# Attention exponents turned in 32x32 blocks by VectorE and through DRAM, instead of by TensorE

## The reference, cut to what matters

```
s_win = jnp.where(valid, s_win, -jnp.inf)
logits = jnp.concatenate([sink_logits(sink, s_win.shape[:-1]), s_ctx, s_win], axis=-1)
p = jax.nn.softmax(logits, axis=-1)
p_ctx = p[..., 1:1 + C].astype(v.dtype)
p_win = p[..., 1 + C:].astype(v.dtype)
return (jnp.einsum('bkgqj,bjkd->bqkgd', p_ctx, v_ctx)
        + jnp.einsum('bkgqj,bjkd->bqkgd', p_win, vw))
```

## Time and profile before

| | |
|---|---|
| median of 3 runs (range) | 1417.44 us (1417.28 to 1417.67) |
| profiled execution, span from first to last instruction | 1416.2 us |
| the runs' median less that span | 1.2 us |
| the attention with the z projection, first scores to last attended block | 383.8 to 657.8 us |
| busy over the whole span: TensorE, weight load, VectorE, ScalarE | 98%, 82%, 61%, 36% |
| mean granted TensorE clock | 0.999 of full speed |

### The profile page before, as it was taken

How to read it: one execution, slowest core, us unless ns; L and a number is a source line. 1 busy time by engine, 2 the same in 40 slices (tenths; PEclk the granted TensorE clock), 3 DMA queues, 4 the chain that set the end, 5 groups by cost and what they waited for, 6 DMA issues and landing times.

```text
span 1416.2 us, 19552 instructions
## 1 busy us (share of the span) xinstructions
PE 1389.8 (98%) x7474; PEld 1166.9 (82%) x7474; DVE 861.2 (61%) x1359; ACT 515.2 (36%) x798; POOL 74.6 (5%) x144
## 2 busy tenths in 40 slices
PE   4999999999999999999999999999999999999998
PEld 2788888888888888888888888888888888887887
DVE  6545655656778676776546685677666334474434
ACT  5323422244556444454222342122363223323332
POOL 0001111011100000000100101000000000010000
PEclk9999999999999999999999999999999999999999
DMA  9996567656712121224766656356523333365323
GB/s 384 407 390 245 184 212 243 195 183 207 223 46 64 56 75 52 67 89 132 234 188 190 197 181 214 92 165 193 177 90 105 92 102 91 106 203 182 111 89 119
DMA packets 64169, 232.75 MB, mean 164 GB/s; under 512 B 7120, under 2 KB 8144, under 8 KB 62816
## 3 DMA queue, kind: packets, MB, share of 16 engines
q1 hardware_dynamic: 42624, 154.23, 32.8%
q0 software_dynamic: 19792, 72.39, 16.3%
q10 hardware_dynamic: 1680, 5.10, 1.1%
HBM read 227.50 MB, written 4.19 MB: 164 GB/s over the span
## 4 chain that ended last, share of the span: by engine, by line
PE 92%; DVE 3%; DMA 2%; ACT 2%; SPq 1%; issue 1%; POOL 0%; POOLq 0%; DVEq 0%; ACTq 0%
PE ps L1439 90%; PE ps L1668 2%; DMA kvmem<-in_ctxT 1%; DMA modchunk<-in_modb 1%; DVE w_lo L857 1%; SPq L370 0%; ACT w_hi L452 0%; DVE modchunk L863 0%; ACT scratch L557 0%; DVE kvmem L1038 0%; PE ps L1793 0%; DVE pt_lo L1174 0%; ACT pt_hi L668 0%; ACT main L801 0%; DVE main L957 0%
## 5 line engine op out<-in xcount | busy, mean ns | idle before, releaser
L1439 PE MATMUL ps<-h_hi,w_hi 128*128 128x512 f32 x1592 | 625.8, 393 | 2.2 <-DVE w_lo L857 1.2
L1439 PE MATMUL ps<-h_hi,w_lo 128*128 128x512 f32 x1592 | 618.8, 389 | 0.0
L1439 PE MATMUL ps<-h_lo,w_hi 128*128 128x512 f32 x1592 | 618.4, 388 | 0.0
L857 DVE TENSOR_TENSOR w_lo<-raw,w_hi 128x1024 fp32r<-128x1024 f32 x206 | 252.3, 1225 | 372.3 <-ACT w_hi L452 372.0
L452 ACT CAST w_hi<-raw 128x1024 fp32r<-128x1024 f32 x206 | 216.1, 1049 | 600.2 <-PE ps L1439 599.9
L1439 PEld LDWEIGHTS ps<-h_hi,w_hi 128*128 128x128 f32 x1592 | 299.0, 188 | 65.7 <-issue 4.7
L1439 PEld LDWEIGHTS ps<-h_hi,w_lo 128*128 128x128 f32 x1592 | 298.9, 188 | 62.8
L1439 PEld LDWEIGHTS ps<-h_lo,w_hi 128*128 128x128 f32 x1592 | 299.2, 188 | 58.7
L863 DVE CUSTOM_DVE_ANT_0 modchunk<-modchunk,cond_row 128x1024 f32<-128x1024 f32 x128 | 154.6, 1220 | 22.2 <-DMA modchunk<-in_modb 22.0
L408 POOL DMA_DIRECT2D modchunk<-in_modb x128 | 67.9, 530 | 1114.9 <-DVE modacc L863 1090.9
L668 ACT CAST pt_hi<-ps 128x512 fp32r<-128x512 f32 (+1 forms) x48 | 30.7, 640 | 110.7 <-PE ps L1668 110.7
(11 more groups left out here) (232 smaller groups left out, 1364.5 us busy)
## 6 DMA issues: line engine op xcount, KB each, us to landing
raw<-in_weights SPq DMA_DIRECT2D x208, 512.0 KB, 3.6
modchunk<-in_modb POOLq DMA_DIRECT2D x128, 512.0 KB, 4.7
raw<-in_mod SPq DMA_DIRECT2D x32, 512.0 KB, 9.0
modchunk<-in_mod SPq DMA_DIRECT2D x16, 512.0 KB, 7.4
cond_row<-in_mod SPq DMA_DIRECT2D x16, 512.0 KB, 8.8
main<-in_xT SPq DMA_DIRECT2D x4, 1024.0 KB, 8.3
main<-in_xT ACTq DMA_DIRECT2D x4, 1024.0 KB, 5.0
out<-pooled SPq DMA_DIRECT2D x16, 256.0 KB, 2.8
```

The lines of the kernel that those rows point to most:

```text
L857: nc.vector.tensor_tensor(low, src, high.bitcast(F32), ALU.subtract).then_inc(lo_ready, 1)
L1439: return nc.tensor.matmul(out, lhsT, rhs, start=start, stop=stop, skip_group_check=True)
```

## The change

- TensorE's `turn` is gone, with the identity matrix and its load. In its place VectorE turns the exponents in 32x32 blocks (`turn_blocks`) into `blocks_out`; SP stores them to a DRAM buffer (one transfer of 128 rows of 2048 or 2560 bytes), waits until the store has landed, and fetches them back with four transfers, so that the 32x32 blocks come to their places of the full transpose (each 32 partitions with four runs of 512 or 640 bytes). High and low parts are then made from SBUF (`turned_hi`, `turned_lo`), three slots after the exponent (`TURN_LAG = 3`) instead of one.
- The exponents are not multiplied with the reciprocal of their sum. The row sums of a query block are inverted together (`invert_sums`, 128x3), sent through DRAM and fetched back as a row broadcast to all partitions, and the attended block is multiplied with it when it is copied out of PSUM (`block_out`).
- A head has 16 slots. `attend` is in the slots 6, 9, 12 and 15, with one bank unit ahead of it, and none behind the last. The next head's keys are prepared in slot 12 and its first scores are made in slot 14. The loops over heads are written out.
- `cond_row` and a part of `modchunk` serve as block buffers. POOL stores one row of `cond_row` to DRAM, and fetches it back to all partitions after the last step; chunk loads wait for that and for the last attended block, and the eight jobs of the first output group are spread as 0, 1, 1, 1, 2, 1, 1, 1.
- Beside the last head 8 of 16 input tiles are split instead of 12. Swaps and rotations of the last query tiles are moved into the first two heads, and reloads of x are later.

```diff
+SLOTS = 16
+UNIT_SLOTS = (2, 4, 6, 8, 10, 12, 13)
+BANK_STEPS = (2,) * 11 + (3, 3, 2, 2, 0)
+BLOCK_SLOTS = (6, 9, 12, 15)
+TURN_LAG = 3
+NEXT_KEYS, NEXT_SCORES = 12, 14
...
+            def store_blocks(i, k):
+                g, cols = i * STEPS + k, key_tiles(k) * P
+                sp.wait_ge(turned, g + 1)
+                sp.dma_start(turn_scratch[g % 4, :, 0:cols], blocks_out[g % 2][:, 0:cols]).then_inc(written[g % 2], 16)
+
+            def fetch_blocks(i, k):
+                g, cols = i * STEPS + k, key_tiles(k) * P
+                run = cols // 4
+                sp.wait_ge(written[g % 2], 16 * (g // 2 + 1))
+                if g >= 2:
+                    sp.wait_ge(pt_ready, g - 1)
+                for j in range(4):
+                    sp.dma_start(blocks_in[g % 2][j * QUADRANT:(j + 1) * QUADRANT, 0:cols].rearrange("c (a x) -> c a x", a=4),
+                                 turn_scratch[g % 4, :, j * run:(j + 1) * run].rearrange("(a c) x -> c a x", a=4)
+                                 ).then_inc(pt_landed[g % 2], 16)
...
+            for i in range(KV_HEADS):
+                for k in range(SLOTS):
+                    if 1 <= k <= STEPS and (k > 1 or i == 0):
+                        fetch_blocks(i, k - 1)
+                    if 3 <= k <= STEPS and k % GQA == 0:
+                        fetch_inverse(i, k // GQA - 1)
+                    if k < STEPS and (k or i == 0):
+                        store_blocks(i, k)
+                    if k < STEPS and k % GQA == GQA - 1:
+                        store_inverse(i, k // GQA)
...
+                    if k in UNIT_SLOTS:
+                        load_unit((G_Z + i) * HALVES + UNIT_SLOTS.index(k) + 6)
...
-            def probabilities(i, k):
-                par = k % 2
-                dve.wait_ge(exp_done, i * STEPS + (k + 1))
-                chain.link(nc.vector.reciprocal(stat[:, 3, par:par + 1], stat[:, 2, par:par + 1]))
-                p = probs[par][:, 0:score_width(k) - 1]
-                nc.vector.tensor_scalar(p, p, stat[:, 3, par:par + 1], None, ALU.mult).then_inc(probs_ready, 1)
+            def turn_blocks(i, k):
+                g, cols = i * STEPS + k, key_tiles(k) * P
+                dve.wait_ge(exp_done, g + 1)
+                if g >= 2:
+                    dve.wait_ge(written[g % 2], 16 * (g // 2))
+                nc.vector.transpose(blocks_out[g % 2][:, 0:cols].rearrange("p (j t c) -> p j t c", j=4, c=QUADRANT),
+                                    probs[k % 2][:, 0:cols].rearrange("p (t j c) -> p j t c", j=4, c=QUADRANT)).then_inc(turned, 1)
...
+            def block_out(i, n):
+                b = i * BLOCKS + n
+                dve.wait_ge(pv_done, b + 1)
+                dve.wait_ge(inverse_landed[b % 2], 16 * (b // 2 + 1))
+                nc.vector.tensor_tensor(main[:, i * GQA + FG:(i + 1) * GQA + FG, n * P:(n + 1) * P],
+                                        ps[:, 7, P:512].rearrange("p (j q) -> p j q", j=GQA),
+                                        inverse_rows[b % 2].rearrange("p (q j) -> p j q", j=GQA), ALU.mult).then_inc(y_done, 1)
...
-            def turn(i, k):
-                pe.wait_ge(probs_ready, i * STEPS + (k + 1))
-                if k and k % GQA == 0:
-                    pe.wait_ge(y_done, i * BLOCKS + k // GQA)
-                for t in range(score_width(k) // P):
-                    ins = nc.tensor.transpose(ps_flat[:, 6 * 512 + t * P:6 * 512 + (t + 1) * P],
-                                              probs[k % 2][:, t * P:(t + 1) * P], ident)
-                ins.then_inc(turned, 1)
```

More of the change, by code:

```diff
@@ L388, in _, with load_units @@
                 load(weights[HALVES + j], j)
[L389 to L392, removed]
+            def load_units(first, end):
+                with sp.Fori(first, end) as q:
+                    for j in range(RAW_SLOTS):
+                        sp.wait_ge(lo_ready, q * RAW_SLOTS + (HALVES + j + 1 - RAW_SLOTS))
+                        load(weights[q * RAW_SLOTS + (HALVES + j)], j)
@@ L393, in _ @@
+            after_heads = G_O * HALVES + 6
+            for u in range(after_heads, after_heads + 2):
+                load_unit(u)
+            load_units(after_heads // RAW_SLOTS - 1, (G_END - 1) * HALVES // RAW_SLOTS)
             for t in range(0, KT, 2):
@@ L698, in attention @@
-                if not last:
-                    exponent(i + 1, 0)
+                    act.wait_ge(turned, (i + 1) * STEPS)
+                    for m in range(GROUP):
+                        tanh_bank(i + B_Z, i * GROUP + T_MIX0, m)
+                else:
+                    for m in range(1, GROUP):
+                        tanh_bank(i + B_Z, i * GROUP + T_MIX0, m)
                     hi(i + G_Z, HALVES + 1)
@@ L705, in _ @@
             place_sink(0, 0)
-            attention(0, first=True)
-            with act.Fori(1, KV_HEADS - 1) as i:
+            for i in range(KV_HEADS):
                 attention(i)
-            attention(KV_HEADS - 1, last=True)
+            for t in range(2 * EARLY_PAIRS, EARLY):
+                split(H_MIX0 + t, main[:, t], h_hi[:, t])
             hi(G_O, 2)
@@ L1205, in attention @@
                     gate_tile(i, 2)
-                    maximum(i + 1, 0)
                     gate_tile(i, 3)
-                    probabilities(i + 1, 0)
                     lo(i + G_Z, HALVES + 1)
-            dve.wait_ge(attn_landed, 48)
-            attention(0, first=True)
-            with dve.Fori(1, KV_HEADS - 1) as i:
-                chain.loop(i, STEPS, first=1)
+            dve.wait_ge(attn_landed, 32)
+            dve.wait_ge(row_stored, 16)
+            for i in range(KV_HEADS):
                 attention(i)
-            chain.end(KV_HEADS - 2)
-            attention(KV_HEADS - 1, last=True)
+            for t in range(2 * EARLY_PAIRS, EARLY):
+                split(H_MIX0 + t, main[:, t], h_hi[:, t], h_lo[:, t])
             lo(G_O, 2)
```

282 lines of the change are left out of this document (179 added, 103 removed).

## The result

| kernel | median us | range (runs) |
|---|---|---|
| before | 1417.56 | 1417.28 to 1417.86 (4) |
| changed | 1445.94 | 1442.52 to 1450.20 (4) |

The ratio is 1.0203, 95% interval 1.0189 to 1.0216: 2.0% slower, where 1396 us, 1.5% faster, was forecast. The profiled execution of the changed kernel took 1450.2 us, its span is 1448.5 us.

The account below looks back on a forecast made before the run. TensorE was taken to pace the attention: span 1416.2 less 23.3 us of transposes plus 2 of stall gives 1394.9, and the median 1.2 above it 1396 us, 1.5% faster. Own range 1394 to 1400 us; chance 0.68.

Parts of the forecast that it names:

- TensorE's transposes, 23.3 us: In the attention, TensorE loses 216 transposes, 0.43 us in each four-tile and 0.54 in each five-tile step: 23.3 us off.
- the rival that read 272 ns as cost: On TensorE, each transpose costs its whole duration, so 59 us come off and the kernel takes 1358 us; chance 0.01.
- VectorE's transposes, 0.73 and 0.87 us from the low bound: VectorE's block transposes of 512 and 640 columns take 0.73 and 0.87 us; upper bound 1.27 and 1.59.
- VectorE becomes the bound: Rival: VectorE's transposes take the upper bound, 0.63 us more each, slowing the attention to 1406 us; chance 0.15.
- Stall of 2 us in all, the tight queue and the seams: TensorE stalls 0.5 us per head behind VectorE's queue between heads, 2 us in all; seams cost 0, at most 1.
- The trip's terms: DRAM round trip of turned blocks: store 3.0 us, fetch 4.0 with four issues holding SP 1.3, 7.0 in all.
- Behind SP's waits only weight loads are queued: free.: In SP's queue, only weight loads with some eight slots until use stand behind the waits, so these cost nothing.
- the exponent's own way round in three slots: Loop of transpose, trip, high part, exponent and semaphores: 9.9 us, fitting TensorE's 10.9 in a head's opening and 13.5 later.
- the trip through DRAM sets the pace: slower: Rival: ScalarE waits ahead of the high part, trip 13.0 us, 38 us lost, 1432 us; decides from about 12.1; chance 0.10.
- Gain and trip cancel: Rival: a three-slot loop of 15.0 us in the attention leaves the kernel at 1415 to 1420 us; chance 0.04.
- Transfers in the attention move only 75 GB/s together: Argument that transfers in the attention are light, 75 GB/s, with weight units landing in 3.6 us, against a slow DRAM trip.
- The rest of the kernel should not move: Outside the attention, from first scores to G_O's first matmul, times should stay as they were.

Follow-up runs that it names:

- e3: The changed kernel without the trip through DRAM: VectorE's turned blocks are read straight from its buffers, blocks off the diagonal not moved to their places; 1396.34 us.
- e2: The changed kernel with SP's order in a slot turned round, the store of step k ahead of the fetch of step k-1; 1406.15 us.
- e14: e2 with each weight unit loaded during the four heads cut from 512 to 64 KB; 1396.99 us.
- e13: The changed kernel with each weight unit loaded during the four heads cut from 512 to 64 KB, SP's order kept; 1424.96 us.
- e7: The changed kernel with one fetch of all 128 rows in place of four, blocks coming back where they were stored; 1413.74 us.
- e9: The changed kernel with each fetch cut into eight transfers of 16 rows instead of four of 32; 1507.24 us.
- e6: The changed kernel with the four heads' weight units issued by ScalarE's queue, one unit slot later; 1468.92 us.
- e8: e2's order, store ahead of fetch, together with e6's weight units on ScalarE's queue, against the changed kernel; 1418.56 us.
- e1: The changed kernel with the 48 stores of turned blocks issued by POOL's queue instead of SP's; 1408.13 us.
- e5: The changed kernel with the fetches of turned blocks issued by POOL's queue, stores and weight units staying on SP; 1432.28 us.
- e12: e2 with two of each fetch's four transfers issued by POOL; 1406.64 us.
- e11: e2 with the inverse sums' store and broadcast issued by POOL's queue; 1412.41 us.

## Why the prediction was wrong, step by step

- **TensorE's transposes, 23.3 us: right.** e3 has them gone, two more bank units in its stage (2.75 us), and stands 254.8 us against 273.9: 19.1 + 2.75 = 21.9 us, and 23.3 less e3's waits of 1.4 is the same. Distances between starts, not durations, were the price; the rival that read 272 ns as cost falls.
- **VectorE's transposes, 0.73 and 0.87 us from the low bound: right.** The changed kernel's line:

```profile
L1274 DVE STREAM_TRANSPOSE cond_row<-kvmem x24: 702/780/847, 388.9 to 670.1; 128x512 f32<-128x512 f32 x12, 128x640 f32<-128x640 f32 x12
L1295 DVE TENSOR_TENSOR main<-ps,modchunk x16: 652/668/682, 412.4 to 692.8; 128x384 f32<-128x384 f32 x16
```

  The second row is the attended block's multiplication, which I priced at the copy's 0.56 us: 0.67 measured, 1.7 us over 16, hidden in e3. VectorE is busy 198.7 of 308.3 us, and 196.9 of 255.2 in e3 (77%; 201 of 251 was forecast). The rival "VectorE becomes the bound" falls.
- **Stall of 2 us in all, the tight queue and the seams: right** where the trip is away or hidden (1.4 us in e3). The weight split that waits in the changed kernel (9.5 us, `w_lo` at L971) stands in VectorE's order behind low parts that wait for a late high part; without the trip it is 0.8 us (e3).
- **The trip's terms: nearly right, 7.6 us for 7.0.** The issues and landings, as the earlier trace rows, then the landings of one store (L421) and of one of a fetch's four transfers (L430):

```profile
blocks<-cond_row SPq DMA_DIRECT2D x24, 320.0 KB, 4.2
blocks<-cond_row SPq DMA_DIRECT2D x24, 256.0 KB, 3.2
...
L421 SPq DMA_DIRECT2D blocks<-cond_row x48: 326/430/983, 389.7 to 681.7; - x48
DMA to landing us min/median/max: 2.1/3.6/8.8
...
DMA to landing us min/median/max: 1.8/2.2/6.1
```

  Store 3.6 us in place of 3.0 (2.1 to 8.8). Fetch, from the first issue to the last landing, 3.7 us in place of 4.0 (medians of the 48 steps; 3.2 to 7.4). Trip 7.6 in place of 7.0 (5.5 to 12.4); the one in the chain above, 399.38 to 408.57, is the longest of the first head, 9.2. An issue that stands alone takes 0.33 us as in the earlier trace rows, but one behind another 0.43 and a gap of 0.04, so four hold SP 1.74 us, not 1.3.
- **The step that failed: "Behind SP's waits only weight loads are queued: free."** The next step's store is queued there too. I checked one loop, the exponent's own way round in three slots (9.9 us, 10.5 with the measured trip, so it fits as I said), and not the loop that SP's order makes in one slot: a landing, four issues and a store's issue, 3.5 + 1.9 + 0.4 = 5.8 us on the mean, against 3.65 and 4.5 us of TensorE. With my own terms, 3.0 + 1.3 + 0.33 = 4.6, it would have been above the opening's 3.65 and level with the later 4.5: the loop would have shown, but only part of its price. e2 shortens no transfer and moves two lines, and 40 of the 50 us are back: that is the proof of which loop it was.
- **The rival "the trip through DRAM sets the pace: slower"** had the place (ScalarE's wait ahead of the high part) and the sign, and 1432 against 1446. Its mechanism and its point of decision were wrong: it wanted a trip above 12.1 us, and the trip is 7.6, so the near number is luck. "Gain and trip cancel" rested on the same loop and falls with it.
- **"Transfers in the attention move only 75 GB/s together", used against that rival: wrong.** The trip itself brought it to 162 GB/s and a DMA share of 0.59, and a weight unit in this stage lands in 5.5 us on the median, not in 3.6. e14 against e2 prices it: 9 us in the good order; e13 21 in the other.
- **No step had the clock.** Three windows of the changed kernel (columns as in the earlier trace rows) and TensorE's timeline there:

```profile
423.00:426.00 3.00, 0.65 (x3) 0.19 (x1) 0.28 (x1) 1.04 (x2) 0.00 (x0) 0.96 0.67 181
426.00:428.00 2.00, 1.41 (x4) 1.41 (x5) 1.01 (x2) 1.98 (x5) 0.00 (x0) 0.50 0.91 286
428.00:430.00 2.00, 2.00 (x8) 2.00 (x8) 1.91 (x3) 0.81 (x2) 0.00 (x0) 0.50 0.54 161
```

```profile
426.60 0.69 PE L1575 MATMUL ps<-pt_hi,v_hi 128*128 128x384 f32 x1 [2.94 <-DVE pt_lo L1287]
427.08 0.52 PE L1575 MATMUL ps<-pt_lo,v_hi 128*128 128x384 f32 x1
427.40 0.52 PE L1575 MATMUL ps<-pt_hi,v_lo 128*128 128x384 f32 x1
```

  TensorE waited 2.94 us; then the granted clock is 0.50, the lower of its two levels (1.2 GHz), and the matmuls stand 0.32 us apart, where they do 0.17 us apart at 1.00 (2.4 GHz). So a gap can be paid twice: of the 52 us against e3 36.3 are waits and about 12 this. Not every gap is: behind a wait of 2.52 us that ended at 409.97 the granted clock stayed at 1.00 to 415.
- **"The rest of the kernel should not move": right** but for 1.8 us. From the last attend to the end it is 755.9 us against 758.4, of which 2.75 are the bank units moved into the heads. The first scores begin at 385.71 instead of 383.87; I found no cause, and e2, e3 and e13 begin them at 382.9 to 383.4.

## What to carry to other kernels

A queue that waits for a landing blocks everything behind it: for each wait on SP, POOL or an engine's queue, list the next issue of the *same pipeline* behind it, and compare landing plus issues with the pace of one step, not only the whole trip with its buffers. Put a round trip's stores ahead of the fetch that waits for the store before. With that (e2, 1406 us) the change beats both kernels, and what is left, 10 us, belongs to the weight traffic beside it. From there on the length of the round trip counts, so look at the landings again before moving transfers to another queue.

## What the runs showed of the hardware

- The time of an issue depends on what stands ahead of it on its queue: 0.32 to 0.34 us alone, 0.43 plus 0.04 right behind another, on SP (e2, e7); 0.54 on POOL.
- With a fetch of 256 or 320 KB cut into eight instead of four transfers the landings were shorter (each eighth 1.9 us, the stores 2.8 and 2.3 instead of 4.2 and 3.2), and the kernel lost 61 us to issues (e9). Whether the cut or the slower pace shortened them, no run tells.
- A store of 256 or 320 KB has medians of 2.1 to 2.9 us with weight units of 64 KB beside it (e13, e14) and of 3.2 and 4.2 with units of 512 KB; the longest landings are 7.9 (e13) and 8.8 us. Issuing the units from another engine made the kernel slower twice (e6, e8).
- In every run that moved a part of the transfers from SP to a second queue a fetch took longer from its first issue to its last landing, on the median: 3.7 us in the changed kernel against 4.5 (e6), 5.5 (e1) and 6.2 (e5); 4.3 in e2 against 5.3 (e8, e12) and 5.5 (e11). Why, and whether the moment of issue or the queue does it, no run shows.
- The Trainium skill ("DMA: Bandwidth & Descriptors", Rules for kernel authors, the row on a DMA that reads what an earlier one wrote) asks for just such a wait on the completion semaphore before the dependent issue. The traces show what the wait costs by its place: 124.7 us at SP with the next store behind it, 29.8 with the store ahead.
